# Weighing an attention head's values one block later, and taking its outputs during the next head

## The reference

```
def block(qi):
    s = jnp.einsum('bqhmd,bkhmd->bhmqk', qi.astype(F32), kf) * scale
    pr = jax.nn.softmax(s, axis=-1)
    pd = pr[:, :, 0] - lam * pr[:, :, 1]
    return jnp.einsum('bhqk,bkhe->bqhe', pd, vf)
...
o = _rmsnorm(o, p["da_gsub"], 1e-5) * (1.0 - lam_init)
y = o.reshape(B, L, DA_VW) * jax.nn.silu(gate.astype(F32))
```

## Time and profile before

| | |
|---|---|
| median of 3 runs | 2750.89 us (2749.11 to 2752.49) |
| profiled execution | 2752.66 us, of which the span is 2750.9 |
| PE busy | 2527.5 us, 92% of the span |
| DVE busy | 1204.0 us, 44% |
| ACT busy | 799.4 us, 29% |
| POOL busy | 564.5 us, 21% |
| mean granted clock of PE | 0.963 of full speed |

### The profile page before, as it was taken

One profiled execution on the slowest core, in us unless ns is written; L12 is line 12 of the kernel. 1 busy time (PEld: TensorE's weight loads), 2 busy tenths in 40 slices (PEclk: granted clock), 3 DMA queues, 4 the chain that ended last, 5 costly groups with the idle time before them and its releaser, 6 DMA issues. The chain is left out here.

```text
span 2750.9 us, 58600 instructions
## 1 busy us (share of the span) xinstructions
PE 2527.5 (92%) x25144; PEld 1699.7 (62%) x25144; DVE 1204.0 (44%) x2168; ACT 799.4 (29%) x1514; POOL 564.5 (21%) x505
## 2 busy tenths in 40 slices
PE   5989997899899999999979999978998989999999
PEld 2547664566676767666545576645766666666665
DVE  3763426463736373221147534264645464632111
ACT  3221424443434342101022214155333333320110
POOL 1223220122222221111022322202131313121110
PEclk9999998999999999999999999999999999999999
DMA  6111121010101010321531121301010101012131
GB/s 260 46 44 60 62 84 46 24 34 27 35 27 35 27 35 28 107 69 63 191 136 54 35 69 50 126 1 39 25 37 24 39 19 42 20 69 81 61 107 69
DMA packets 41944, 165.64 MB, mean 60 GB/s; under 512 B 5184, under 2 KB 5184, under 8 KB 40160
## 3 DMA queue, kind: packets, MB, share of 16 engines
q1 hardware_dynamic: 35856, 131.09, 14.2%
q0 software_dynamic: 5840, 30.87, 2.9%
HBM read 149.88 MB, written 12.06 MB: 59 GB/s over the span
## 5 line engine op out<-in xcount | busy, mean ns | idle before, releaser
L729 PE MATMUL ps<-scr 32*32 32x32 f32 (+9 forms) x17704 | 679.6, 228 | 90.3 <-issue 31.7
L729 PEld LDWEIGHTS ps<-scr 32*32 32x32 f32 (+5 forms) x17704 | 523.4, 123 | 287.0 <-issue 232.3
L783 PE MATMUL ps<-x,ring 128*128 128x320 f32 x1184 | 363.7, 449 | 25.7 <-DVE scr L2051 22.6
L729 PE MATMUL ps<-h,ring 128*128 128x320 f32 x1184 | 366.6, 452 | 21.1 <-ACT h L1638 17.8
L783 PEld LDWEIGHTS ps<-x,ring 128*128 128x128 f32 x1184 | 225.8, 196 | 125.9 <-issue 46.2
L729 PEld LDWEIGHTS ps<-h,ring 128*128 128x128 f32 x1184 | 225.3, 197 | 122.9 <-issue 32.3
L2051 DVE TENSOR_TENSOR scr<-ps,scr 128x320 f32<-128x320 f32 x174 | 84.3, 490 | 445.8 <-PE ps L729 277.8
L587 POOL TENSOR_TENSOR ring<-ring,sums 128x512 f32<-128x512 f32 x66 | 90.7, 1374 | 763.0 <-PE ps L729 674.9
L1587 ACT ACTIVATE scr<-ps 128x320 f32<-128x320 f32 x174 | 75.5, 435 | 388.3 <-PE ps L729 289.7
L729 PE MATMUL ps<-h,sums 128*128 128x320 f32 x592 | 175.8, 437 | 0.2
L783 PE MATMUL ps<-h,ring 128*128 128x320 f32 x592 | 175.9, 438 | 0.0
(11 more groups left out here) (281 smaller groups left out, 2960.2 us busy)
## 6 DMA issues: line engine op xcount, KB each, us to landing
ring<-in_w SPq DMA_DIRECT2D x240, 512.0 KB, 3.5
spill<-x POOLq DMA_DIRECT2D x8, 640.0 KB, 3.3
scr<-spill POOLq DMA_DIRECT2D x2, 2560.0 KB, 9.6
x<-in_x SPq DMA_DIRECT2D x1, 2560.0 KB, 16.3
yc<-in_win POOLq DMA_DIRECT2D x2, 1280.0 KB, 8.7
x<-in_x POOLq DMA_DIRECT2D x2, 1280.0 KB, 7.8
out_y<-x POOLq DMA_DIRECT2D x8, 320.0 KB, 6.5
x<-out_y POOLq DMA_DIRECT2D x2, 1280.0 KB, 8.1
```

Source lines behind the costliest of these rows:

```text
L729: return nc.tensor.matmul(out, lhsT, rhs, start=start, stop=stop)
L783: return nc.tensor.matmul(out, lhsT, rhs, start=False, stop=stop, skip_group_check=True)
```

## The change

On PE `weigh` moves from behind the transposes of q = 3 to behind those of q = 4, right ahead of `weigh_ctx`. On ACT both `outputs` of a head move behind the exponentials of the next head's block q = 1, ahead of the copy of its block q = 0; the last head's stand at the end of the stage. DVE's program is as it was.

```diff
@@ -1129,9 +1129,8 @@
                         scores(u + 2)
                     hd_, q = units[u]
                     turn_pd(u)
-                    if q == 3:
+                    if q == 4:
                         weigh(hd_)
-                    if q == 4:
                         weigh_ctx(hd_)
 
                 def head_sums(hd_):
@@ -1791,10 +1790,13 @@
                 for u in range(len(units)):
                     exps(u)
                     if u >= 1:
+                        hd_, q = units[u - 1]
+                        if q == 0 and hd_ >= 1:
+                            outputs(2 * hd_ - 2)
+                            outputs(2 * hd_ - 1)
                         turned_pd(u - 1)
-                        if units[u - 1][1] >= 3:
-                            outputs(2 * units[u - 1][0] + units[u - 1][1] - 3)
                 turned_pd(len(units) - 1)
+                outputs(2 * HEADS - 2)
                 outputs(2 * HEADS - 1)
                 act.wait_ge(o_ready, 2 * HEADS)
                 i_l = ORDER.index(("lora",))
```

## The result

The changed kernel takes 2733.54 us in the median of four runs (2732.36 to 2738.28) against 2751.69 for the kernel before, a ratio of 0.9934 with an interval of 0.9913 to 0.9955. It is faster, by about 18 us where 12.7 were forecast. Its profiled execution took 2738.28 us, the longest of the four, with a span of 2736.5.

A forecast was written before the change was run, and what follows sets the result against it. Hand-overs between engines, none full, were taken to bound the attention stages. Six changes of head at 1.92 us (11.5) plus 1.2 for last heads gave 12.7 us: median 2738.2 us, range 2730 to 2746.

The forecast's parts named there:

- The order of a change of head: PE, DVE, ACT between heads: next head's q1' scores come early, PE's waits vanish, DVE's 5.43 us wait becomes 3.4 at q2'.
- the cover of the outputs: ACT's output copies finish 0.8 us before PE's transposes of the next head's first block, q0', need them.
- The price of 1.92 us: Gain per change of head, maxima of q2' starting at 448.58 instead of 450.50; six changes give 11.5 us.
- rival A: More gain: half-clock stretch no longer falls on the scores of q0'; 2731.7 us; chance 0.06 for this or better.
- The first half of rival B: Scores of q1' run at half clock, costing 0.95 us per change of head; rival B overall 2749.7 us, chance 0.11.
- the second half of B: Some 1 us worth of the weighing at half clock costs 1 us more, eating the 1.92; same rival, chance 0.11.
- Rival C: Slower: the whole weighing between heads runs at half clock, 2.48 us lost six times; 2764.6 us; chance 0.05.
- The last head: End of each layer's attention: q4's copy beside the weighing, outputs following each other, 0.58 us earlier; two layers 1.2.
- the sum: Whole forecast gain: 11.5 us from six changes of head plus 1.2 from the last heads, 12.7 us.
- all six weighings between heads ran at full clock: PE's weighings in the kernel before, read from its profile: the row of 5.84 us stands six times.

The follow-up runs named there:

- The two halves alone: Kernel before with only PE's weighing moved behind q4: 2757.38 us, ratio 1.0017; kernel before with only ACT's outputs moved into the next head: 2755.59 us, ratio 1.0005.
- the split kernel: Changed kernel with the weighing cut into pieces between later blocks' scores, and ACT's outputs behind the exponentials of q2': 2726.07 us, ratio 0.9898 against the changed kernel.

## Why the prediction was right, and where its size was off

**The order of a change of head** was right step for step. The scores of q1' start with no pause after the transposes of q3, the maxima of q1' follow q4, both waits of PE are gone, the remaining wait stands at the maxima of q2' with 3.15 us where 3.4 were worked out, and ACT waits 1.62 us for the weighing where 1.7 were. That the cover of the outputs holds is seen in the transposes of q0', which start right behind the scores. The two halves alone, with ratios of 1.0017 and 1.0005, show that each of the waits hid the other.

**The price of 1.92 us** is 1.84 where the clock is nearly full in both kernels. The first profiles of the two kernels as they are give the same on average: from the maxima of q4 in a layer's first head to those in its last, DVE takes 62.27 and 61.76 us before and 55.84 and 57.17 after, 11.0 us less for six changes of head. Single heads scatter, from 17.48 to 19.55 us in the changed kernel's first profile; their mean is 18.8, in its second profile 18.7, where the prediction had 18.9 and the first profile of the kernel before 20.7. The scatter comes from the half-clock stretch, which still falls on the scores of q0' in nearly every head (2.51 and 2.37 us in the second and third change of layer 0). In the first head of layer 0 it did not (1.35, the row at 437.56 above): rival A happened once in the 12 changes of the two profiles. The first half of rival B happened in five of them: the scores of q1' took 1.59 to 1.89 us and DVE's maxima of q1' waited 0.31 to 0.61 for them. That reached as far as those scores and no further. The weighing ran at full clock in all 12, so neither the second half of B nor C came about.

**The last head** was forecast to give 0.58 a layer. In layer 0, from the end of ACT's copy of q3 to the next stage, it went from 513.23 - (502.05 + 0.70) = 10.48 to 505.53 - (496.19 + 0.70) = 8.64 us. Of these 1.8 the weighing's clock is most: 7.57 us before, and now 6.49 with the context weighing in the same row. In layer 1 it went from 9.13 to 8.75, 0.4 us. The first row here is of the kernel before, the others of the changed one:

```profile
502.05 0.70 ACT L1771 ACTIVATE scr<-ps 128x640 f32<-128x640 f32 x1 [0.78 <-PE ps L1107]
...
496.19 0.70 ACT L1770 ACTIVATE scr<-ps 128x640 f32<-128x640 f32 x1 [1.27 <-PE ps L1107]
...
503.58 0.60 ACT L1778 ACTIVATE yc<-ps 128x512 f32<-128x512 f32 x1 [5.78 <-PE ps L729]
504.07 0.27 ACT L1780 ACTIVATE yc<-ps 128x128 f32<-128x128 f32 x1
504.38 1.06 ACT L1804 ACTIVATE lora<-ring 128x1024 f32<-128x1024 f32 x1
...
505.53 2.39 PE L729 MATMUL ps<-h,ring 128*128 128x320 f32 x8 [1.77 <-issue]
```

**What was mis-sized** is the base of the sum. Against the profile that it was made from, the sum holds: 11.0 us where 11.5 were forecast for the changes of head, 2.2 where 1.2 were for the last heads, 13.2 in all for the 12.7. But "all six weighings between heads ran at full clock" was read from one profile and taken for the kernel's habit. In three further profiles with the old order on PE six of 18 did not, and the kernel before's stages, 181.5 us in that first profile, take 184.1 and 190.8 in the other two: 185.5 on average, against 168.3 and 167.9 in the changed kernel. So the stages give 17.3 us rather than 12.7, as far as three profiles that lie 9 us apart can say. The clock takes from both orders, but more from the old one: filling the pauses shortens its stages by 12.5 us (185.5 to 173.0) and those of the new order by 8.7 (168.1 to 159.5). The difference of 3.8 us is what lies between the 13.5 us of the order by itself and the 17.3. Rival C had the sign turned round: it is the old order whose weighing is at risk. No experiment was made on that alone. What the rows show is that before the weighing PE used to stand 0.80 us after scores and transposes, and now works through another 1.35 us of scores first, and that from the same state the old order's weighing stayed at half clock six times in six and the new order's never in three.

**The rest.** By the larger samples the medians lie 21.8 us apart, the stages 17.3. The 4.5 us between are open. Outside the two stages the span is 2569, 2572 and 2561 us in the three profiles of the kernel before and 2568 and 2563 in the two of the changed one, and 2563 to 2580 in the other kernels, whose work there is the same; a few profiles can't settle 4.5 us in that. The profile with the longest stages, 190.8 us, is the one with the 2561 outside them, and its run was the faster of the two later ones: the stages alone don't explain how the runs of the kernel before scatter. That the gain is not handed back later is settled by the medians.

## What to carry to other kernels

Where three engines pass blocks round, look for the long piece of work that stands between two engines' hand-overs, and ask of each engine's queue what is held up behind it: here PE's scores and ACT's exponentials were both held up by the same 4.4 us of weighing, and moving one of them alone gained nothing. A stall that has moved one block on is worth following again: splitting the long piece took another 8 us or so, though by the rows only some 3 of them through the hand-over and the rest through the clock. And price a kernel whose clock changes from more than one profile: the first one can show the favourable case.

## What was not expected of the hardware

The half-clock stretches fall elsewhere in each execution of the same program. In three profiles of the kernel before a weighing between heads, with the scores behind it, took 5.84 us or 7.50 to 7.81, the longer in none, one and three of six, and its 28 runs spread over 2746.6 to 2765.6 us, while the six of the split kernel lie within 5.1 us. Three matmuls a head whose results nobody reads, put where PE would have stood, made the kernel before 11 us faster (0.9956) with a clock of 0.99 from 440 to 500 us, where it was 0.93, 0.92 and 0.88 in the three profiles of the plain kernel. The mean clock of a stretch doesn't price it, though: in the changed kernel, whose stages are shorter, it was 0.87 and 0.89 there.
